# Feed-forward part of a decoder layer: seven block products in place of eight for 18 of 22 column blocks, and a down-projection stage of its own

## What is computed

```python
h = _rmsnorm(x, pre_g)                   # 1024 columns
g = h @ w_gate                           # 1024 x 2816
u = h @ w_up                             # 1024 x 2816
gp = jnp.concatenate([prev, g], axis=1)
c = conv_b
for j in range(3):
    c = c + conv_w[j] * gp[:, j:j + S]
a = jax.nn.gelu(c, approximate=True) * u
out = a @ w_down                         # 2816 x 1024
return x + _rmsnorm(out, post_g), gp[:, -2:]
```

## Time and profile before

| | us |
|---|---|
| runs, median (lowest to highest) | 1608.21 (1605.41 to 1611.03) |
| the profiled execution's own time | 1607.8 |
| its span in the trace | 1605.6 |
| PE busy (share) | 1491.0 (93%) |
| weight loads of PE busy (share) | 1340.4 (83%) |
| DVE busy (share) | 694.8 (43%) |
| POOL busy (share) | 571.9 (36%) |
| ACT busy (share) | 541.8 (34%) |

### The profile page before, as it was taken

The page is one execution under the profiler, slowest core; times in us unless marked ns, Lnnn a source line. Parts: engine busy times, 40 slices in busy tenths (PEclk is TensorE's granted clock), DMA queues, the critical chain, the costliest instruction groups (busy, mean ns, idle before and its releaser), DMA issues. The chain is left out here.

```text
span 1605.6 us, 25434 instructions
## 1 busy us (share of the span) xinstructions
PE 1491.0 (93%) x9919; PEld 1340.4 (83%) x9919; DVE 694.8 (43%) x1258; ACT 541.8 (34%) x1079; POOL 571.9 (36%) x391
## 2 busy tenths in 40 slices
PE   3999789999999899779999999999999999999995
PEld 3989667777768676467779999999999999999994
DVE  4320375676554444454541434143342433424245
ACT  5543445554343344353433211203122131211212
POOL 3211565554533420122233523325242242422314
PEclk9899899999999999999999999999999999999997
DMA  5112455677756554321231211112111120201024
GB/s 185 27 40 57 134 172 185 209 224 236 226 187 194 179 186 165 124 75 58 93 96 58 74 33 53 40 40 66 40 53 40 40 66 25 68 27 40 27 82 159
DMA packets 155944, 164.02 MB, mean 102 GB/s; under 512 B 19947, under 2 KB 108331, under 8 KB 155787
## 3 DMA queue, kind: packets, MB, share of 16 engines
q1 hardware_dynamic: 155824, 162.40, 32.0%
HBM read 144.19 MB, written 18.26 MB: 101 GB/s over the span
## 5 line engine op out<-in xcount | busy, mean ns | idle before, releaser
L1277 PE MATMUL PS<-ht_hi,wgu_hi 128*128 128x344 f32 x1056 | 337.4, 319 | 0.8 <-PEq L1361 0.8
L1277 PE MATMUL PS<-ht_lo,wgu_hi 128*128 128x344 f32 x1056 | 336.9, 319 | 0.0
L1277 PE MATMUL PS<-ht_hi,wgu_lo 128*128 128x344 f32 x1056 | 336.9, 319 | 0.0
L1304 POOL TENSOR_TENSOR wgu_lo<-wgu_raw,wgu_hi 128x1024 fp32r<-128x1024 f32 x44 | 105.8, 2405 | 341.4 <-ACT wgu_hi L1300 341.3
L1069 PE MATMUL PS<-ht_hi,w_hi 128*128 128x344 f32 x576 | 198.8, 345 | 20.6 <-DVE ht_lo L826 10.8
L560 POOL TENSOR_TENSOR k_page<-k_page,q_bc 128x1024 f32<-128x1024 f32 x64 | 153.2, 2399 | 170.6 <-DMA k_page<-in_cache_fox_k 142.0
L1824 DVE SCALAR_TENSOR_TENSOR conv<-gate,conv_consts,conv 128x1024 f32<-128x1024 f32 x44 | 80.0, 1817 | 308.7 <-ACT conv L1767 307.9
L1277 PEld LDWEIGHTS PS<-ht_hi,wgu_hi 128*128 128x128 f32 x1056 | 198.6, 188 | 0.9 <-issue 0.8
L1277 PEld LDWEIGHTS PS<-ht_hi,wgu_lo 128*128 128x128 f32 x1056 | 198.4, 188 | 0.0
L1277 PEld LDWEIGHTS PS<-ht_lo,wgu_hi 128*128 128x128 f32 x1056 | 198.1, 188 | 0.0
L1069 PE MATMUL PS<-ht_hi,w_lo 128*128 128x344 f32 x576 | 189.5, 329 | 0.0
(11 more groups left out here) (221 smaller groups left out, 2489.1 us busy)
## 6 DMA issues: line engine op xcount, KB each, us to landing
k_page<-in_cache_diff_k SPq DMA_DIRECT2D x64, 256.0 KB, 3.1
k_page<-in_cache_fox_k SPq DMA_DIRECT2D x64, 256.0 KB, 3.8
v_page<-in_cache_diff_v SPq DMA_DIRECT2D x64, 256.0 KB, 2.7
v_page<-in_cache_fox_v SPq DMA_DIRECT2D x64, 256.0 KB, 2.9
w_raw<-in_w_in SPq DMA_DIRECT2D x24, 512.0 KB, 4.6
wgu_raw<-in_w_gate SPq DMA_DIRECT2D x22, 512.0 KB, 3.8
wgu_raw<-in_w_up SPq DMA_DIRECT2D x22, 512.0 KB, 3.8
wd_raw<-in_w_down SPq DMA_DIRECT2D x44, 256.0 KB, 2.8
```

What stands on the lines that cost most here:

```text
L1277: ins = pe.matmul(PS[:, bank, 0:THIRD], w[:, slot, k, :], a[:, k, i * THIRD:(i + 1) * THIRD], start=(k == 0 and n == 0), stop=(k == KC - 1 ...
L1304: pool.tensor_tensor(w_lo[:, q % WR, :, :], raw[:, q % 2, :, :], w_hi[:, q % WR, :, :].bitcast(F32), ALU.subtract).then_inc(gu_lo, 1)
```

## The change

The gate and up products of blocks 4 to 21 are made as one product of a 2x2 block matrix by another, with seven block products and sums around them (Strassen's scheme in Winograd's form). The input rows are halved (chunks 0 to 3, 4 to 7), the tokens too (two halves of 516), and the columns are gate and up. A block product is 4 x 3 x 2 = 24 matmuls of 258 tokens; seven are 168 matmuls in place of 144 of 344 tokens.

- Sums of tokens (t2, t3, t4 and t1, which takes the place of a quarter of ht_hi and ht_lo) are made once by DVE and split by ACT and DVE beside the first four blocks, which stay as before (`plain`).
- Sums of weights are made per block by DVE (`sums`: four of 128x512, both inputs in SBUF), in the place of raw weights. ACT splits seven slots in place of four (1024, 1536 and 1024 columns), POOL takes their low parts in three instructions of those sizes.
- Five combinations per block (`combine`) on DVE read PSUM and a copy p1 of product 0 or an earlier combination. Products 3, 5 and 6 add on in PSUM to what a combination must have read before.
- Up now goes to SBUF (ubuf), and DVE multiplies there. The product a is stored to DRAM (a_dram), no longer split at once.
- The down-projection follows as a stage of 88 steps: all f for the first third, then the second, then the last third in two halves of four output blocks. It sums over all 22 blocks in PSUM, in 8 banks, so the 264 additions in SBUF go; 24 cells are copied out by ACT and DVE. w_down is loaded once for each third (5 slots ahead), a comes back from DRAM by thirds. ACT makes high parts, DVE low parts (both inputs in SBUF).
- Five of the nine turns are made within the last third's first half, four behind it.

The core of the diff:

```diff
+PLAIN = 4
+HALF = TOK // 2
+PIECE = HALF // 2
...
+            def sums(f):
+                loaded(dve, f)
+                if f - 2 >= PLAIN:
+                    dve.wait_ge(prod_done, prods(f - 2, 6))
...
+                dve.tensor_tensor(s3, a11, a21, ALU.subtract).then_inc(sum_step, 1)
...
+                dve.tensor_tensor(s1, a21, a22, ALU.add).then_inc(sum_step, 1)
...
+                dve.tensor_tensor(s2, s1, a11, ALU.subtract).then_inc(sum_step, 1)
...
+                dve.tensor_tensor(s4, a12, s2, ALU.subtract).then_inc(sum_step, 1)
...
             for f in range(FC):
+                n = f + 1
+                if f > PLAIN:
+                    combine(f - 1, GATE2)
...
+                if PLAIN <= n < FC:
+                    sums(n)
+                if f:
+                    conv(f - 1, 1)
+                if f >= PLAIN:
+                    combine(f, U2)
+                if f:
+                    conv(f - 1, 0)
+                    multiply(f - 1)
+                if f >= PLAIN:
+                    for e in (U3, UP2, UP1):
+                        combine(f, e)
...
+                    pool.wait_ge(sum_step, 4 * (n - PLAIN) + 4)
+                    pool.wait_ge(gu_hi, weight_parts(n, 0))
+                    split_lo(pool, n, A11, A12 + 1)
+                    pool.wait_ge(gu_hi, weight_parts(n, 1))
+                    split_lo(pool, n, S2, S4 + 1)
+                    pool.wait_ge(gu_hi, weight_parts(n, 2))
+                    split_lo(pool, n, S1, A22 + 1)
...
+            def product(f, n):
...
+                for k in range(4):
+                    for m, (w, a) in enumerate(((w_high, a_high), (w_high, a_low), (w_low, a_high))):
+                        for piece in range(2):
+                            ins = pe.matmul(PS[:, bank + piece, 0:PIECE], w[:, k, :], a[:, k, piece * PIECE:(piece + 1) * PIECE],
...
+            def strassen(f):
...
+                product(f, 0)
...
+                product(f, 1)
+                pe.wait_ge(act_done, 2 * (f - PLAIN) + 1)
+                product(f, 2)
+                pe.wait_ge(evac_done, evacs(f, U2))
+                product(f, 3)
...
+                product(f, 4)
+                pe.wait_ge(evac_done, evacs(f, U3))
+                product(f, 5)
+                pe.wait_ge(evac_done, evacs(f, UP2))
+                product(f, 6)
...
+            def down(s):
+                p, f = sub(s), f_of(s)
+                pe.wait_ge(down_low, split_parts(s))
+                for d in d_of(p):
...
+                    for m, (w, a) in enumerate(((wd_hi[s % NW], a_hi[f]), (wd_hi[s % NW], a_lo[f]), (wd_lo[s % NW], a_hi[f]))):
+                        ins = pe.matmul(PS[:, cell_bank(p, d), 0:THIRD], w[:, c], a[:, :],
+                                        start=f == 0 and m == 0, stop=f == LAST and m == 2, skip_group_check=True)
```

More of the change, by code:

```diff
@@ L1608, in ffn @@
     bias = cst[:, :, 2 * DB + 3]
-    e = 0
-    sq = place.at(e, "y_squares", D); e += 4 * D
-    OS = 4
[L1613 to L1617, removed]
+    NW = 5
+    wd_at = lambda s: R_SETS + 8 * D * (s % NW) if s % NW < 2 else R_SETS + SET_BYTES + 8 * D * (s % NW - 2)
@@ L1632, in ffn @@
[L1632 to L1638, removed]
+    row_in, stored = io["row_in"], [sem(f"stored{s}") for s in range(OS)]
+    a_stored = [sem("a_stored0"), sem("a_stored1")]
@@ L1697, in _ @@
+            for t in range(EARLY, NS):
+                store_y(t)
+            sp.wait_ge(conv_stored, 48)
             for s in range(OS):
@@ new lines, in _ @@
+            combine(FC - 1, GATE2)
+            for s in range(STEPS):
+                low_weights(s)
+                if s == 4:
+                    conv(FC - 1, 1)
+                    conv(FC - 1, 0)
+                if s == 6:
+                    multiply(FC - 1)
+                if s > FC and f_of(s) == LAG - 1:
+                    evacuate(sub(s) - 1)
+                for t in range(EARLY):
+                    if s == turn_step(t) + LAG + 2:
+                        norm(t)
+            evacuate(3)
@@ L1911, in _ @@
                 ins.then_inc(tt_done, 1)
-            down(NG - 1)
-            for t in range(FIRST, NS):
+            for f in range(PLAIN):
+                for up in range(2):
+                    plain(f, up)
+                    if f == 0 and not up:
+                        pe.wait_ge(rows_ready, 48)
+                        for n in range(FC):
+                            ins = pe.transpose(PS[:, 6, n * NR:(n + 1) * NR], rows_in[0:NR, n * P:(n + 1) * P], ident[0:NR, 0:NR])
+                        ins.then_inc(cst_t, 1)
+            for f in range(PLAIN, FC):
+                strassen(f)
+            pe.wait_ge(cst_done, 1)
+            for s in range(STEPS):
+                for n in range(6):
+                    if s == TAIL_STEP + n // 2 * 2:
+                        turn_tails(n)
+                for t in range(EARLY):
+                    if s == turn_step(t):
+                        turn(t)
+                down(s)
+            for t in range(EARLY, NS):
                 turn(t)
```

700 lines of the change are left out of this document (463 added, 237 removed).

## The result

| | before | after |
|---|---|---|
| median of the runs (lowest to highest), us | 1608.81 (1605.41 to 1611.03) | 1643.6 (1641.62 to 1646.8) |
| the profiled execution: time, span | 1607.8, 1605.6 | 1643.51, 1641.7 |
| ratio after/before, 95% interval | | 1.022 (1.0195 to 1.0245) |

The change makes the kernel 34.8 us slower, where 16 were forecast: the sign was right, and the time lies 3.6 us above the range.

The account below looks back on a forecast made before the run. PE alone was taken to bound the kernel before. Span 1605.6 + 1.8 (11.3 - 4.3 + 3 + 2 - 10.2 at full clock) + 14.4 for the clock = 1621.8; time 1624 us, range 1598 to 1640.

Parts of the forecast that it names:

- PE's own saving: Blocks of seven products: 258-token matmuls take 0.120 us, so a block is 20.2 us in place of 22.6.
- The block's chain: Blocks of seven products: DVE and POOL exclude each other, PE waits 3 us before product 5, a block takes 23.0 us.
- Block 4: First block of seven products: the sum of t1 stands ahead of the weight sums, so it takes 27.7 us.
- the last one: Last block of seven products: no sums behind it, a 2.5 us pause before the down stage, 22.6 us.
- The clock: Pauses before product 5: half of 18 followed by 3.4 us at half clock, 9 x 1.6 = +14.4 us.
- The plain blocks: First four blocks: matmuls kept, token sums and ACT's splits fit in PE's 83 us, so 0.
- The down stage: Down-projection: same matmuls, 0; +3 us (0 to +20) for loads in the last third; +2 for turns inside.
- rival D: Down stage: last third bound by its loads, 22 steps each 0.5 to 1 us longer, 1642 us (1636 to 1655); chance 0.10.
- The end: Behind the last down matmul: four turns left in place of seven, 16.2 us in place of 26.4, -10.2.
- C: Blocks of seven products: not slower, PE sets the pace at 20.2 us a block, 1558 us, partly up to 1603; chance 0.20.

Follow-up runs that it names:

- Experiment 4: Changed kernel plus 12 spare matmuls of 258 columns in blocks 4 to 21, ahead of the wait for U3: 1622.39 us.
- experiment 5: Changed kernel with a semaphore of its own for gate's first weights, so ACT's first high part waits for gate's load alone: 1633.51 us.
- nopool: Also called experiment 2: changed kernel with POOL's three subtractions in blocks 4 to 21 made copies of 4 columns, low part of weights left out: 1560.95 us.
- plain20: Changed kernel with 20 plain blocks and 2 of seven products in place of 4 and 18: 1607.4 us, ratio 1.0 to the kernel before.
- after2: The changed kernel run once more, unchanged: median 1637.59 us.
- experiment 3: Changed kernel with DVE's two 8-column operations moved ahead of the two large taps, right behind the weight sums: 1581.04 us, ratio 0.9807 to the kernel before.
- experiments 7 and 9: 7: changed kernel, U3 ahead of the multiplication, 1614.04 us. 9: 8-column operations early, gate's own semaphore, block 4 reordered, 1579.72; with two load orders, 1580.39 and 1574.04.
- experiment 8: Changed kernel with the next weight loads ahead of the store of the activations in the DMA queue, in every block: 1657.29 us.

## Why the prediction was right in kind and short in size

- **PE's own saving**: right. Matmuls of 258 tokens start 0.1205 us apart (I took 0.120), and where nothing else sets the pace a block is 20.24 us (20.2). The load of 128 weight columns stays hidden at this size too; by the rule of the Trainium skill that I had weighed against it (TensorE: Matmul & The Clock Gate, LDWEIGHTS and Part 3, The mechanism) the estimate was 0.215. The measurement decides against that rule. The same section of the Trainium skill also lets a load into a background weight buffer go ahead of running matmuls, and the rows fit that.
- **The block's chain**: right step by step: U3 at 17.2 in the mean (17.4), sums 1.1 (0.9), U2 8.1 (8.0). **The failing step is the last addition in it.** PE is ready at 14.2 and U3 comes at 17.4, a wait of 3.2 that I rounded to 3; from 17.4, products 5 and 6 and their latency, 5.76 + 0.2, make 23.36. I wrote 23.1 and then used 23.0. Experiment 4 has 23.43 with the clock at 1.00. The 0.43 us that each of 16 blocks lacks, 0.36 of it this slip, make 6.9 us, half of what the forecast lacks when the spread is taken off.
- **Block 4** 27.6 (27.7), and the last one with its pause 22.8 (22.6): right. In block 4 the two half-clock stretches lie ahead of U3, which ends at 21.6 and so sets the start of product 5: they cost nothing.
- **The clock**: the term was right, its makeup not. 9 x 1.6 = 14.4 against 15.5 measured, but from more stretches that cost less each, since part of each lies in the pause: 12 stretches in blocks 5 to 20, 1.3 each. That the sum came so near is in part luck: I had no row for how many there would be. The one behind the pause ahead of the down stage belongs to this term as well and is counted below. The trace before also had two pauses of 1.6 and 1.7 us (ending at 419.6 and 669.4) with 0.50 behind them, which I had overlooked.
- **The plain blocks**, taken as 0, cost 1.4 (96.1 against 94.7), of which about 1 is the half-clock stretch behind the merge.
- **The merge** was not in the sum at all: the moved wait (ACT's first high part now waits for gate's and up's load) costs 2.2 us, shown by experiment 5. I had followed every wait inside the FFN and none ahead of it.
- **The down stage**: 261.6, where my sum, less the other stages, left 259.5. Up to 1.7 of the 2.1 is the half-clock stretch at its start; where there is none, the stage takes 260.3 (nopool) and 260.1 (plain20). PE waits inside it for 2.9 us in all, so rival D, a stage bound by its loads, did not come, although ACT waited 107.8 us for the activations and 34.6 for w_down.
- **The end**: 16.0 (16.2): right.

Sum of what was missing: 6.9 + 1.1 (clock) + 1.4 + 2.2 + 2.1 - 0.2 = 13.5. With it the forecast span of 1621.8 becomes 1635.3, beside after2's 1635.7; the first profile's 1641.7 has 6.4 of spread on top. Of the rivals, C (PE sets the pace) gave 1558 for the case that DVE and POOL get by each other: experiment 2, which makes that case, had 1560.95. It was a good price for a condition that was not met, and experiment 3 shows that a reordering of two small operations meets it in all of these blocks but the first, block 4.

## What to carry to other kernels

Where VectorE, with both inputs in SBUF, and GpSimd work at once, the length of an instruction says little: here one of 8 columns behind GpSimd subtractions took 2.2 us in the mean, where a subtraction of 1024 columns alone takes 2.4. Put the short ones where GpSimd is idle. When work is moved on one engine, look for the DMA queue that waits for it: twice here (experiments 7 and 9) a store waiting for the moved multiplication held back the weight loads behind it. Add the chain up twice, and price PE's pauses with the half-clock stretch behind them, which here cost nearly a third as much again as the waits (15.5 against 16 x 3.2 us).

## What I had not expected of the hardware

- **Pauses and clock.** Over the blocks of seven products and the pause behind them, in the twelve profiles of the changed kernel and its variants, the clock fell to 0.50 behind 1 of 25 pauses of PE of 1.1 to 1.8 us, behind neither of 2 of 2.2 to 2.3, behind 54 of 76 of 2.4 to 3.2, and behind all 11 that were longer. In the plain blocks and the down stage it fell behind 1 of 16 pauses of 1.1 to 2.0. Pauses of one length go both ways, as the two shown above do.
- **A small delay grows.** In experiment 8, 0.2 us more of pause went with 23 stretches in place of 15, and with 13 us in the blocks. That the longer pause is the cause was not tested by itself; two profiles of after, with the same code, had 15 and 16 stretches.
- **The stage ahead.** The same instructions, up to the merge, took from 687.6 to 702.9 us over twelve profiles. A difference of 5 us between two kernels needs their profiles side by side, from a common mark on, and even then the same blocks differed by 3.8 us between two profiles (experiment 5).
